# A two-layer hybrid block on one core: convolutions, rotary products and gelu dealt to GpSimd, VectorE's steps in a new order, the first loads in turn

## The reference, cut to what matters

```python
def reference(x, norm_mix, w_in, ...):
    for l in range(DEPTH):
        h = rms_norm(x, norm_mix[l])
        proj = h @ w_in[l]
        (dq, dk, dv, dz, da, db, mq, mk, mv, lx, ly, gates) = split_columns(proj)
        ...
def gated_deltanet(q, k, v, z, a, bb, conv_w, a_log, dt_bias, norm_w):
    qkv = jax.nn.silu(causal_depthwise_conv(jnp.concatenate([q, k, v], axis=-1), conv_w))
    ...
def rg_lru_branch(xb, yb, conv_w, conv_b, w_r, b_r, w_i, b_i, lam):
    xc = causal_depthwise_conv(xb, conv_w) + conv_b.astype(xb.dtype)
    ...
    return (hs * jax.nn.gelu(yb.astype(jnp.float32))).astype(xb.dtype)
```

## Time and profile before

| | |
|---|---|
| median of 3 runs | 966.09 us (965.6 to 966.27) |
| the profiled execution | 965.97 us, its span 964.1 us |
| TensorE busy | 924.6 us, 96% |
| VectorE busy | 686.6 us, 71% |
| ScalarE busy | 469.9 us, 49% |
| GpSimd busy | 0.2 us |
| mean granted TensorE clock | 0.996 |
| DMA | 159.69 MB, mean 166 GB/s |

### The profile page before, as it was taken

The page is one execution under the profiler, slowest core; times in us unless marked ns, Lnnn a source line. Parts: engine busy times, 40 slices in busy tenths (PEclk is TensorE's granted clock), DMA queues, the critical chain, the costliest instruction groups (busy, mean ns, idle before and its releaser), DMA issues.

```text
span 964.1 us, 15474 instructions
## 1 busy us (share of the span) xinstructions
PE 924.6 (96%) x6432; PEld 837.9 (87%) x6432; DVE 686.6 (71%) x1079; ACT 469.9 (49%) x747; POOL 0.2 (0%) x4
## 2 busy tenths in 40 slices
PE   4998999999999999999999899999999999999995
PEld 3997998999988888888889899999999888888884
DVE  4999976796767555555579998759758675555555
ACT  5554253875345444444454633558644454444441
POOL 0000000000000000000000000000000000000000
PEclk9999999999999999999999999999999999999998
DMA  8543433466565656565644344334655565555541
GB/s 330 168 147 126 135 105 119 131 190 195 169 196 164 198 179 197 175 203 188 202 134 134 127 133 132 123 119 134 217 188 182 176 197 196 186 179 193 179 137 44
DMA packets 44133, 159.69 MB, mean 166 GB/s; under 512 B 5024, under 2 KB 5024, under 8 KB 43936
## 3 DMA queue, kind: packets, MB, share of 16 engines
q1 hardware_dynamic: 44064, 158.72, 50.6%
HBM read 157.65 MB, written 1.05 MB: 165 GB/s over the span
## 4 chain that ended last, share of the span: by engine, by line
PE 83%; DVE 13%; DMA 1%; ACT 1%; SPq 1%; issue 1%; DVEq 0%; ACTq 0%
PE bank L277 11%; PE bank L278 10%; PE bank L279 10%; PE bank L340 8%; PE bank L342 8%; PE bank L341 8%; PE bank L390 6%; PE bank L319 5%; PE bank L318 5%; PE bank L317 5%; DVE wlo L834 3%; DVE tmp L877 3%; DMA par<-params_dram 1%; DVE proj L920 1%; PE bank L355 1%; PE bank L379 1%
## 5 line engine op out<-in xcount | busy, mean ns | idle before, releaser
L623 ACT CAST whi<-raw 128x1024 fp32r<-128x1024 f32 x292 | 305.6, 1049 | 384.7 <-PE bank L279 152.7
L834 DVE TENSOR_TENSOR wlo<-raw,whi 128x1024 fp32r<-128x1024 f32 x292 | 353.2, 1219 | 113.8 <-ACT whi L623 113.6
L277 PE MATMUL bank<-ahi,whi 128*128 128x256 f32 x896 | 259.7, 290 | 14.0 <-DVE wlo L834 13.3
L278 PE MATMUL bank<-alo,whi 128*128 128x256 f32 x896 | 254.4, 284 | 0.0
L279 PE MATMUL bank<-ahi,wlo 128*128 128x256 f32 x896 | 254.2, 284 | 0.0
L277 PEld LDWEIGHTS bank<-ahi,whi 128*128 128x128 f32 x896 | 172.6, 193 | 16.4 <-DVE wlo L834 13.3
L278 PEld LDWEIGHTS bank<-alo,whi 128*128 128x128 f32 x896 | 172.8, 193 | 0.1
L279 PEld LDWEIGHTS bank<-ahi,wlo 128*128 128x128 f32 x896 | 172.7, 193 | 0.0
L340 PE MATMUL bank<-whi,ahi 128*128 128x512 f32 x352 | 139.2, 395 | 1.6 <-DVE alo L892 1.6
L342 PE MATMUL bank<-whi,alo 128*128 128x512 f32 x352 | 137.3, 390 | 0.0
L341 PE MATMUL bank<-wlo,ahi 128*128 128x512 f32 x352 | 137.1, 389 | 0.0
(11 more groups left out here) (217 smaller groups left out, 1113.9 us busy)
## 6 DMA issues: line engine op xcount, KB each, us to landing
raw<-stream_dram SPq DMA_DIRECT2D x292, 512.0 KB, 4.1
par<-params_dram SPq DMA_DIRECT2D x2, 600.5 KB, 10.2
proj<-xt_dram SPq DMA_DIRECT2D x4, 256.0 KB, 3.9
x<-x_dram SPq DMA_DIRECT2D x1, 1024.0 KB, 11.8
out_dram<-x SPq DMA_DIRECT2D x4, 256.0 KB, 2.3
con<-consts_dram SPq DMA_DIRECT2D x1, 676.0 KB, 12.6
proj<-final_dram SPq DMA_DIRECT2D x1, 512.0 KB, 6.3
nrm<-norms_dram SPq DMA_DIRECT2D x1, 16.0 KB, 1.8
```

Of the source, the lines that this page charges most:

```text
L277: pe.matmul(dst, whi_of(m)[:, wcol], hi, start=first, stop=False, skip_group_check=True)
L278: pe.matmul(dst, whi_of(m)[:, wcol], lo, start=False, stop=False, skip_group_check=True)
L623: act.copy(whi_of(m), raw_of(m)).then_inc(*AC.up(("hi", m), "w"))
L834: dv.tensor_tensor(wlo_of(m), raw_of(m), whi_of(m), ALU.subtract).then_inc(*DV.up(("lo", m), "w"))
```

## The change

- **GpSimd** gets a program of its own: the convolutions and silus of q (chunks 0, 1) and v (chunks 4, 5), the rotary products, the recurrent convolution, and the gelu path. A fused step of VectorE becomes two GpSimd instructions, a multiply and an add. k (chunks 2, 3) stays on VectorE. New tiles `CB`, `XP` and `GT` hold what is between.
- **The order.** First taps at k = 4, 5, 7, 9, 11, 13, tanh at 7, 9, 9, 11, 15, 17. "grow" goes from k = 8 to 6 and its reader from 9 to 8, "gcol" from 10 to 9, "dif" from 12 to 11 (its transposes from 11 to 10). q is transposed at k = 12, k at 13, v at 20. The steps from "kes" to "inverse", and most of the delta rule and recurrent steps to k = 51, go one half chunk later, on all engines, `Kend`'s reader to k = 17.
- **The start.** The a and b columns get their own tensor and load (`rab`, 64 KB). The order is norm weights, x transposed 0, tile 0, x transposed 1, tile 1, x transposed 2 and 3, `rab`, tiles 2 and 3, x, tile 4, constants, parameters. ScalarE and VectorE split tiles 0 and 1 between the pieces of x transposed. The steps on the parameters go from k = 0 to k = 3. TensorE begins with six 512-column float32 matmuls on zeros.

```diff
-        CONV_AT = (5, 6, 7, 9, 11, 15)
+        TAP_AT, TANH_AT = (4, 5, 7, 9, 11, 13), (7, 9, 9, 11, 15, 17)
+        DV_CONV = {2: 8, 3: 10}
...
             for p in range(4):
                 sp.dma_start(tiles(XT + 2 * p, 2), xt_in[:, 2 * p:2 * p + 2, :]).then_inc(loaded_xt[p], 16)
-            for m in range(RING):
-                load(m)
+                if p < 2:
+                    load(p)
+            sp.dma_start(rab[:, :, :, :], ab_in).then_inc(loaded_ab, 16)
+            load(2)
+            load(3)
             sp.dma_start(x[:, :, :], x_in).then_inc(loaded_x, 16)
+            load(4)
             sp.dma_start(con[:, :], consts).then_inc(loaded_con, 16)
...
+            pe.wait_ge(*DV.at(0, "zeros"))
+            for i in range(6):
+                exact(bank[7][:, :], tmp[:, 0, 0:P], tmp[:, 0, :])
...
-                if k == 16:
+                if k == 17:
                     pe.wait_ge(*AC.at(l, "kend"))
...
+                for c in range(6):
+                    if k == TANH_AT[c]:
+                        act.wait_ge(*conv_of(c).at(l, ("conv", c)))
+                        act.activation(tanh_pair(c), conv_pair(c), ACT.Tanh, scale=0.5).then_inc(*AC.up(("tanh", c)))
...
+        @block.gpsimd
+        def _(po):
...
+            def conv(srcs, dsts, parts, ws, done):
+
+                if PO.n:
+                    settle()
+                for s in (1, 2, 3):
+                    for i in range(2):
+                        if s > 1:
+                            settle(1)
+                        step(po.tensor_scalar(parts[i][:, s:T], srcs[i][:, 0:T - s], p_("conv", ws[i] + 3 - s), None, ALU.mult))
+                    for i in range(2):
+                        settle(1)
+                        step(po.tensor_tensor(dsts[i][:, s:T], dsts[i][:, s:T], parts[i][:, s:T], ALU.add), done)
+
+            def qkv_conv(l, c):
+                po.wait_ge(*AC.at(l, ("tap", c)))
+                conv([proj[:, 2 * c + i, :] for i in range(2)], [conv_tile(c, i) for i in range(2)],
+                     [tanh_pair(c)[:, i * T:(i + 1) * T] for i in range(2)], [TAPS * (2 * c + i) for i in range(2)], ("conv", c))
+
+            def silu(l, c):
+                po.wait_ge(*AC.at(l, ("tanh", c)))
+                step(po.tensor_scalar(tanh_pair(c), tanh_pair(c), 1.0, None, ALU.add))
+                settle()
+                step(po.tensor_tensor(flat(tiles(2 * c, 2)), tanh_pair(c), conv_pair(c), ALU.mult), ("silu", c))
+
+            def rope(l, i):
+                r, s = (tiles(t + 4 * i, 4, slice(0, 32)) for t in (TMQ, ROT))
+                po.wait_ge(*DV.at(l, ("shuffle", i == 1)))
+                step(po.tensor_tensor(r, r, over(c_("cos", 256, slice(0, 32)), 4), ALU.mult))
+                step(po.tensor_tensor(s, s, over(c_("sin", 256, slice(0, 32)), 4), ALU.mult))
+                settle()
+                step(po.tensor_tensor(r, r, s, ALU.add), "rope")
...
+            for l in range(L):
+                PO.layer = l
+                qkv_conv(l, 0)
+                qkv_conv(l, 1)
+                silu(l, 0)
+                silu(l, 1)
+                qkv_conv(l, 4)
+                qkv_conv(l, 5)
+                silu(l, 4)
+                silu(l, 5)
+                rope(l, 0)
+                rope(l, 1)
+                lru_conv(l, 0)
+                lru_conv(l, 1)
+                po.wait_ge(*AC.at(l, "y2"))
+                step(po.tensor_scalar(tiles(GT, 4), tiles(GT, 4), 0.044715, 1.0, ALU.mult, ALU.add))
+                settle()
+                step(po.tensor_tensor(tiles(GT, 4), tiles(GT, 4), tiles(TLY, 4), ALU.mult), "gelu_in")
+                po.wait_ge(*AC.at(l, "gelu_t"))
+                step(po.tensor_scalar(tiles(GT, 4), tiles(GT, 4), 1.0, None, ALU.add))
+                settle()
+                step(po.tensor_tensor(tiles(GT, 4), tiles(GT, 4), tiles(TLY, 4), ALU.mult))
+                settle()
+                po.wait_ge(*DV.at(l, "scan"))
+                step(po.tensor_tensor(tiles(GT, 4), tiles(GT, 4), tiles(HS, 4), ALU.mult), "lru_f")
```

More of the change, by code:

```diff
@@ L88, in last, with build @@
         return self.sem, self.n - back
-def build(nc, wstream, params, consts, norms, final, x_in, xt_in, out, known):
+def build(nc, wstream, params, consts, norms, final, x_in, xt_in, ab_in, out, known):
     ctx = ExitStack()
@@ L430, in side @@
                     ins.then_inc(*PE.up("kT"))
-                if k == 13:
+                if k == 12:
+                    pe.wait_ge(*PO.at(l, ("silu", 1)))
                     for g in range(8):
@@ L449, in side @@
                     ins.then_inc(*PE.up("qk"))
[L450 to L452 removed]
+                if k == 20:
+                    pe.wait_ge(*PO.at(l, ("silu", 5)))
                     for g in range(8):
@@ L630, in x_norm @@
                         act.wait_ge(loaded_nrm, 16)
+                    if first and kt in (2, 4):
+                        hi(kt // 2 - 1)
                     if kt % 2 == 0:
@@ L635, in x_norm @@
                 if first:
-                    for m in range(AHEAD):
+                    for m in range(2, AHEAD):
                         hi(m)
@@ L688, in side @@
                                        scale=p_("conv", TAPS * (12 + t) + 3)).then_inc(*AC.up(("xtap", t // 2)))
[L690 to L695, removed]
-                        act.activation(tmp[:, c % 2, i * T:(i + 1) * T], proj[:, 2 * c + i, :], ACT.Copy,
-                                       scale=p_("conv", TAPS * (2 * c + i) + 3)).then_inc(*AC.up(("tap", c)))
+                for c in range(6):
+                    if k == TAP_AT[c]:
+                        act.wait_ge(*DV.at(l, ("evac", c)))
+                        if c >= 4:
+                            act.wait_ge(*PO.at(l, ("silu", c - 4)))
+                        for i in range(2):
+                            act.activation(conv_tile(c, i), proj[:, 2 * c + i, :], ACT.Copy,
+                                           scale=p_("conv", TAPS * (2 * c + i) + 3)).then_inc(*AC.up(("tap", c)))
                 if k == 28:
@@ L869, in log1p @@
                 step(dv.tensor_scalar(acc, acc, 2.0, None, ALU.mult))
-            def conv(l, srcs, dsts, ws, done):
-                for s in (1, 2, 3):
-                    for i in range(2):
-                        if s > 1:
-                            settle(1)
-                        step(dv.scalar_tensor_tensor(out=dsts[i][:, s:T], in0=srcs[i][:, 0:T - s], scalar=par[:, ws[i] + 3 - s:ws[i] + 4 - s],
-                                                     in1=dsts[i][:, s:T], op0=ALU.mult, op1=ALU.add), done)
             def x_add(l, step_name, k, t, c):
@@ L889, in x_norm @@
                 for kt in range(KT):
+                    if name == "mix" and l == 0 and kt in (2, 4):
+                        lo(kt // 2 - 1)
                     if kt % 2 == 0:
@@ L1229, in _ @@
             DV.layer = 0
+            step(dv.memset(tmp[:, 0, :], 0.0), "zeros")
             step(dv.memset(inv[upper, :, 0:SUB], 0.0))
             x_norm(0, "mix", 0)
-            for m in range(AHEAD):
+            for m in range(2, AHEAD):
                 lo(m)
```

203 lines of the change are left out of this document (102 added, 101 removed).

## The result

The changed kernel takes **1002.95 us** (median of 4 runs, 1002.83 to 1004.66) against 966.13 for the kernel before (4 runs, 965.6 to 966.27): ratio 1.0379, 95% interval 1.0367 to 1.0392. It is 3.8% slower. 956.3 was predicted, so the forecast has the wrong sign, and the time lies 30 us beyond the upper end of the range.

A forecast was written before the change was run, and what follows sets the result against it. TensorE was taken as the bound, busy 924.6 of 964.1 us. 965.97 - 1.1 (start) - 12.0 (waits) = 952.9, plus 3.4 for sharing, gave 956.3 us; range 950.5 to 973.

The forecast's parts named there:

- The waits that go: TensorE's waits on `grow` (3.7 us), `Kend` (5.9) and `xcopy` (2.4), over both layers, would vanish: -12.0 us.
- The GpSimd step: Each GpSimd multiply or add of the q convolutions was taken as 0.60 us, so convolution 1 ends at 47.1.
- the prediction's own deadlines: GpSimd may end convolution 1 as late as 50.1 at no cost to TensorE; silu(1) is due at 57.
- Sharing: GpSimd stands still for half of VectorE's 8.0 us of two-input steps, 4.0: TensorE waits 1.7 us per layer, 3.4 in all.
- rival B: Full price of sharing SBUF on both engines, 9.6 us per layer: 972.1 us; chance 0.25 for 962 us and up.
- more than 10 us to spare: GpSimd's later deadlines (v's silu by 86, rotary by 110, recurrent convolution by 137) were said to have this margin.
- C: GpSimd by itself at 1.13 us a step, convolution 1 ending at 59.8: 11.8 us per layer, 976.5 us; chance 0.11.
- The half clock after a rest: At the start, TensorE's rest before `wab` halves its clock: +2.2 us, start +1.1 instead of -1.1, forecast 958.5; chance 0.35.
- What would show it wrong: GpSimd steps of 0.9 us or more, tanh(1) ending after 53, or TensorE waiting for silu(1) or silu(3).

The follow-up runs named there:

- run with stand-ins: Changed kernel with each GpSimd step replaced by memsets lasting about its undisturbed time, under the same waits and signals: 964.23 us, 0.9979.
- start alone: Kernel before with only the changed start (load order, separate a and b load, six matmuls on zeros, parameter steps at k = 3): 965.31 us, 0.9992.
- the gelu run: Changed kernel with the five gelu steps of each layer back on VectorE as four, at k = 48 and 50: 992.05 us, 1.0278.
- the run with TensorE kept busy: Changed kernel with seven 512-column float32 matmuls on constants put before half chunk 12 in each layer: 1003.06 us, 1.0391.

## Why the prediction was wrong, point by point

- **The waits that go, -12.0 us: right.** With GpSimd's arithmetic out of the way the kernel takes 952.56 us where the sum gave 952.9, and each layer is 5.8 us shorter where 6.0 were predicted. One wait that the prediction did not find (z's silu, 1.7 us in all) is in that. But the term needs the load off VectorE: with all of it back there, the same order gives 964.3. (The steps up to `grow` that it counts as 22 are 16; their 3.0 us are right.)
- **The GpSimd step, 0.60 us: mis-sized.** Undisturbed, a multiply takes 0.90 and an addition 0.70 (1.82 and 1.42 for two). The step was chosen by VectorE's row of twice the elements, between bounds of 0.41 and 1.13; the mean of 0.80 lies inside them. At 0.80 convolution 1 would end at 51.9, which by the prediction's own deadlines is 1.8 us of waiting per layer. The run with stand-ins costs 11.7 us in all, 6.4 of it in that wait, and most of the 6.4 comes from stand-ins that were too slow. The estimate of 0.56 that the prediction worked out from the Trainium skill's 4497 ns for 2048 elements (GPSIMD Engine Reference, section Performance versus the Vector engine) is below both kinds. Nor would the sum have come out the same with it, as the prediction says: convolution 1 would end 1.0 us earlier, at its deadline, and the sum would be some 2 us lower.
- **Sharing, half of 8.0 us per layer, 3.4 us in all: the step that failed.** It measured 38.7 us at the least. Its full price (rival B) was worked out as 19.2, half of that. Three things were missing. It was counted for the q convolutions and the first rotary step only; the gelu and rotary steps, given "more than 10 us to spare", gave back 10.9 and 5.9 us when taken off GpSimd, almost as much together as q (19.4). VectorE was taken to stand behind half a GpSimd step, while it stood behind nearly whole ones: a split beside a two-input step of 512 elements takes 1.07 us more (2.29), beside one of 1024 elements 2.1 us more (6.67 for two splits). And the margins were GpSimd's; nobody asked what VectorE's delay, in the places without a GpSimd deadline, does to the evacuation or the X chain behind it.
- **Rivals B and C were treated as alternatives.** Each alone gives 972 or 976, but sharing at its full price and steps slower than 0.60 us came together.
- **The half clock after a rest was put at the start only.** It was right there (start alone: nothing gained that can be told). The new rests brought it to other places too: the granted clock is 0.974 in the mean, and 0.995 with no GpSimd arithmetic. Over 1000 us that is some 21 us at full pace, an upper bound: the gelu run is in keeping with 4 to 5 us of it as a real price, the run with TensorE kept busy shows none. At the start it also put off the deadlines that GpSimd had to meet, to 52.1 from 50.1 in the run with stand-ins.
- **What would show it wrong** was named well: steps of 0.9 us, tanh(1) after 53 (it came at 55.95), new waits before half chunk 12. The chances given to it, 0.20 for slower, were too low for two engines on one memory that no row of the trace had ever shown together, with a rule of the Trainium skill against it that the prediction itself cites (SBUF — State Buffer, section Who interferes with whom).

## What to carry to other kernels

Before handing a busy VectorE's work to an idle GpSimd, count the VectorE steps that read two SBUF tensors beside GpSimd's two-input steps, and price each at nearly a whole GpSimd step on top, in every place where the two meet, not only where GpSimd has a deadline. An empty stand-in (memsets under the same waits, of no length and of the true length) takes two runs and tells what the unloading is worth, what the engine's own pace costs, and what sharing costs: here -13.6, at most +11.7 and at least +38.7 us. Read the stand-ins' own length from the trace before the difference is believed; here they were 14% too long. If GpSimd must multiply by a scalar, write two operations, but look at what the faster engine then meets: here 0.4 us saved on each of 72 multiplies, and more on the silus, gave 6.0 us.

## What the hardware showed

- A GpSimd multiply or addition with a scalar takes about twice as long with one operation as with two: 0.86 against 0.42 us for 255 elements, 0.94 against 0.50 with a pointer, 1.49 against 0.79 for an addition on 512.
- VectorE's split of 1.22 us takes 2.25 us in the mean when it meets GpSimd's two-input steps, and 1.21 when it meets only its one-input ones; a GpSimd multiply of 0.93 us took 3.00 beside two splits in a row.
- VectorE's steps of 8 to 12 elements, 0.17 us each, took 0.4 to 0.8 us beside GpSimd's steps of 253 to 255 elements.
- A rest of TensorE of 4.5 us before `wab` and one of 6.0 before half chunk 12 were each followed by a granted clock of 0.5.
